# 96 token slots per expert and pass, and an expert block's four turns set singly between products of its second down item

## What is computed

```python
def swiglu(h, w_gate_up, w_down):
    g, u = jnp.split(h @ w_gate_up, 2, axis=-1)
    return (jax.nn.silu(g) * u) @ w_down

def moe_ffn(h, router, w_gate_up, w_down):
    t = h.reshape(B * S, D)                          # 256 x 1024
    logits = (t @ router).astype(jnp.float32)        # 8 experts
    top_v, top_i = lax.top_k(logits, TOP_K)          # 2 of 8 per token
    gates = jax.nn.softmax(top_v, axis=-1)
    combine = jnp.sum(jax.nn.one_hot(top_i, N_EXPERTS) * gates[..., None], axis=1)
    for e in range(N_EXPERTS):
        out = out + combine[:, e:e + 1] * swiglu(t, w_gate_up[e], w_down[e])
```

## Time and profile before

| | |
|---|---|
| median of three runs | 1441.33 us |
| span of the profiled execution | 1439.5 us |
| TensorE matmul busy | 1433.5 us (100% of the span) |
| VectorE busy | 1140.8 us (79%) |
| ScalarE busy | 964.0 us (67%) |
| GpSimd busy | 97.2 us (7%) |
| read from HBM | 434.88 MB |

### The profile page before, as it was taken

The page is one execution under the profiler, slowest core; times in us unless marked ns, Lnnn a source line. Parts: engine busy times, 40 slices in busy tenths (PEclk is TensorE's granted clock), DMA queues, the critical chain, the costliest instruction groups (busy, mean ns, idle before and its releaser), DMA issues.

```text
span 1439.5 us, 19842 instructions
## 1 busy us (share of the span) xinstructions
PE 1433.5 (100%) x6854; PEld 1205.2 (84%) x6854; DVE 1140.8 (79%) x898; ACT 964.0 (67%) x839; POOL 97.2 (7%) x146
## 2 busy tenths in 40 slices
PE   9999999999999999999999999999999999999999
PEld 9998888888998888888888888888888888888887
DVE  6486654554676698989888888998898898888897
ACT  7465444444684577777777777777777777777775
POOL 3010000000031120000000000000000000000000
PEclk9999999999999999999999999999999999999999
DMA  9454655554345599999999999999999999999995
GB/s 334 142 176 146 220 189 180 199 177 154 106 176 171 202 378 391 375 373 396 383 362 393 392 360 388 395 368 374 394 379 367 393 392 353 396 389 371 380 393 201
DMA packets 212590, 442.92 MB, mean 308 GB/s; under 512 B 16372, under 2 KB 56760, under 8 KB 212544
## 3 DMA queue, kind: packets, MB, share of 16 engines
q1 hardware_dynamic: 208640, 430.18, 81.9%
q0 software_dynamic: 3888, 12.13, 2.8%
q10 hardware_dynamic: 16, 0.00, 0.0%
HBM read 434.88 MB, written 7.37 MB: 307 GB/s over the span
## 4 chain that ended last, share of the span: by engine, by line
PE 99%; DVE 1%; ACT 0%; issue 0%; POOL 0%; DVEq 0%; ACTq 0%; POOLq 0%
PE PS L1716 21%; PE PS L1717 21%; PE PS L1720 21%; PE PS L1421 5%; PE PS L1420 5%; PE PS L1419 5%; PE PS L1150 4%; PE PS L1206 2%; PE PS L1198 2%; PE PS L1200 2%; PE PS L1257 1%; PE PS L1263 1%; PE PS L1260 1%; PE PS L1180 1%; PE PS L1705 1%; PE PS L1708 1%
## 5 line engine op out<-in xcount | busy, mean ns | idle before, releaser
L1862 DVE TENSOR_TENSOR wlo<-ring,whi 128x2048 fp32r<-128x2048 f32 x334 | 764.1, 2292 | 96.5 <-ACT whi L785 94.4
L785 ACT ACTIVATE whi<-ring 128x2048 fp32r<-128x2048 f32 x334 | 640.5, 1919 | 186.5 <-PE PS L1720 176.4
L1716 PE MATMUL PS<-whi,xhi 128*128 128x512 f32 x864 | 340.9, 395 | 0.0
L1717 PE MATMUL PS<-whi,xlo 128*128 128x512 f32 x864 | 336.6, 390 | 0.0
L1720 PE MATMUL PS<-wlo,xhi 128*128 128x512 f32 x864 | 231.0, 389 | 0.0
L1720 PEld LDWEIGHTS PS<-wlo,xhi 128*128 128x128 f32 x864 | 162.1, 188 | 33.9 <-DVE wlo L1862 0.2
L1717 PEld LDWEIGHTS PS<-whi,xlo 128*128 128x128 f32 x864 | 162.4, 188 | 32.3
L1716 PEld LDWEIGHTS PS<-whi,xhi 128*128 128x128 f32 x864 | 162.3, 188 | 32.4
L1716 PE MATMUL PS<-whi,hhi 128*128 128x512 f32 x440 | 172.0, 391 | 0.0
L1717 PE MATMUL PS<-whi,hlo 128*128 128x512 f32 x440 | 171.3, 389 | 0.0
L1829 DVE TENSOR_TENSOR wlo<-ring,whi 128x2048 fp32r<-128x2048 f32 x42 | 96.2, 2292 | 59.0 <-ACT whi L754 59.0
(11 more groups left out here) (380 smaller groups left out, 1584.8 us busy)
## 6 DMA issues: line engine op xcount, KB each, us to landing
ring<-in_moe_w_gate_up SPq DMA_DIRECT2D x448, 512.0 KB, 6.7
ring<-in_moe_w_down SPq DMA_DIRECT2D x224, 512.0 KB, 5.7
ring<-in_dense_w_gate_up SPq DMA_DIRECT2D x56, 512.0 KB, 4.5
ring<-in_dense_w_down SPq DMA_DIRECT2D x28, 512.0 KB, 3.9
ring<-in_a_w_in SPq DMA_DIRECT2D x12, 768.0 KB, 6.2
ring<-in_mem_w_kv SPq DMA_DIRECT2D x4, 1024.0 KB, 5.5
ring<-in_a_w_out SPq DMA_DIRECT2D x4, 1024.0 KB, 5.2
ring<-in_b_w_out SPq DMA_DIRECT2D x4, 1024.0 KB, 4.8
```

The source lines that it names most:

```text
L785: nc.scalar.activation(whi[:, j, :], ring[:, h * SLOT:(h + 1) * SLOT], ACT.Copy).then_inc(S("highs"), 1)
L1716: mm(out_, lhsT=xh, rhs=whi[:, j, c0:c0 + HD], start=begin, stop=False)
L1717: mm(out_, lhsT=xl, rhs=whi[:, j, c0:c0 + HD], start=False, stop=False)
L1862: v.tensor_tensor(wlo[:, j, :], ring[:, h * SLOT:(h + 1) * SLOT], whi[:, j, :].bitcast(F32), ALU.subtract).then_inc(S("lows"), 1)
```

## The change

`CAP` becomes 96, so `PASSES` becomes 3. A few small tiles whose width was `CAP` but that are also used otherwise (`Sx`, `iota`, `first_slot`) keep a width of 128, and the placing of the results (`gates`) handles a third pass with two more small VectorE operations. An expert block's four turns no longer stand behind item 5 but inside it: behind the first matmul of each of the item's four pairs one chunk is turned. The item's first matmul waits for `h_ready` too.

```diff
-CAP = 128
+CAP = 96
...
+            def turn_chunk(c):
+
+                return tr(PS[:, 3, c * CAP:(c + 1) * CAP], hnE[:, c * P:(c + 1) * P])
+
+            def expert_cut(i, b, q, j, parts, turn=None):
...
                 pe.wait_ge(S("highs"), upto(i, PERE, ECUT + m + 1))
-                for out_, xh, xl, c0, begin, end in parts:
+                if turn is not None:
+                    pe.wait_ge(S("h_ready"), turn)
+                for c, (out_, xh, xl, c0, begin, end) in enumerate(parts):
                     mm(out_, lhsT=xh, rhs=whi[:, j, c0:c0 + HD], start=begin, stop=False)
+                    if turn is not None:
+                        turned = turn_chunk(c)
+                        if c == 3:
+                            turned.then_inc(S("h_turned"), 1)
                     mm(out_, lhsT=xl, rhs=whi[:, j, c0:c0 + HD], start=False, stop=False)
...
-                        if last and b == NBE - 1:
-                            expert_down(i, b, b - 1, between=lambda: turn_expert(i * NBE + (NB + NBE)))
-                            continue
-                        expert_down(i, b, b - 1)
+                        expert_down(i, b, b - 1, i * NBE + (NB + b + 1))
                     elif not first:
                         pe.wait_ge(S("h_low"), i * NBE + NB)
-                        expert_down(i, 0, NBE - 1)
-                    if b > 0 or not first:
-                        turn_expert(i * NBE + (NB + b + 1))
+                        expert_down(i, 0, NBE - 1, i * NBE + (NB + 1))
...
+                for q in range(2, PASSES):
+                    then(v.tensor_scalar(place_at[:, 1], place_at[:, 0], float(q * CAP), float((NE - 1) * CAP), ALU.is_ge, ALU.mult))
+                    then(v.tensor_tensor(place_at[:, 2], place_at[:, 2], place_at[:, 1], ALU.add))
```

More of the change, by code:

```diff
@@ L288, in build @@
         o = 2 * NT * FB
-        Sx = carve(o, NT, CAP); o += NT * CAP
+        Sx = carve(o, NT, P); o += NT * P
         tok_f = carve(o, NT); o += NT
@@ L293, in build @@
         NC = PASSES * NE
-        iota = carve(o, CAP); o += CAP
-        iotai = arena[:, o:o + CAP].bitcast(I32); o += CAP
+        iota = carve(o, P); o += P
+        iotai = arena[:, o:o + P].bitcast(I32); o += P
         m8 = carve(o, NT, 8); o += NT * 8
@@ L301, in build @@
         picked = carve(o, NT + 1, NE); o += (NT + 1) * NE
-        first_slot = carve(o, CAP); o += CAP
+        first_slot = carve(o, P); o += P
         key = carve(o, NT); o += NT
@@ L651, in _ @@
             pool.wait_ge(S("att_out"), 1)
-            pool.iota(iotai, pattern=[[1, CAP]], base=0, channel_multiplier=0).then_inc(S("iota"), 1)
+            pool.iota(iotai, pattern=[[1, P]], base=0, channel_multiplier=0).then_inc(S("iota"), 1)
             pool.wait_ge(S("iota"), 1)
@@ L660, in _ @@
             pool.memset(blank[:, :, 0], 0.0).then_inc(S("iota"), 1)
-            pool.tensor_copy(blank[:, :, 1], iota[0:NC + 1]).then_inc(S("iota"), 1)
-            pool.tensor_scalar(blank[:, :, 2], iota[0:NC + 1], float(SEQ), None, ALU.add).then_inc(S("iota"), 1)
+            pool.tensor_copy(blank[:, :, 1], iota[0:NC + 1, 0:CAP]).then_inc(S("iota"), 1)
+            pool.tensor_scalar(blank[:, :, 2], iota[0:NC + 1, 0:CAP], float(SEQ), None, ALU.add).then_inc(S("iota"), 1)
             pool.wait_ge(S("iota"), 8)
@@ L1682, in gather @@
                         last = mm(PS[:, 6 + k // 4, (k % 4) * CAP:(k % 4 + 1) * CAP], lhsT=xn[:, t, k * P:(k + 1) * P],
-                                  rhs=Sx[:, t, :], start=(t == 0), stop=(t == NT - 1))
+                                  rhs=Sx[:, t, 0:CAP], start=(t == 0), stop=(t == NT - 1))
                     if k == KH - 1:
@@ L1693, in _ @@
             more = pe.value_load(cnt_i[0:1, 0:1], min_val=0, max_val=PASSES - 1)
-            def expert_cut(i, b, q, j, parts):
+            def turn_chunk(c):
+                return tr(PS[:, 3, c * CAP:(c + 1) * CAP], hnE[:, c * P:(c + 1) * P])
+            def expert_cut(i, b, q, j, parts, turn=None):
                 m = expert_item(i, b, q)
@@ L1731, in expert_gate_up, with expert_down @@
                          q == 3 and kk == 1) for kk in range(2) for g in range(2)])
-            def expert_down(i, b, f, between=None):
+            def expert_down(i, b, f, turn):
                 for q in (4, 5):
-                    if q == 5 and between:
-                        between()
                     _, _, j = expert_slot(i, b, q)
@@ L1740, in expert_down @@
                         (PS[0:CAP, 4 + hh, :], hhiE[:, 2 * (q - 4) + kk, :], hloE[:, 2 * (q - 4) + kk, :], kk * D + hh * HD,
-                         f == 0 and q == 4 and kk == 0, f == NBE - 1 and q == 5 and kk == 1) for kk in range(2) for hh in range(2)])
+                         f == 0 and q == 4 and kk == 0, f == NBE - 1 and q == 5 and kk == 1) for kk in range(2) for hh in range(2)],
+                        turn=turn if q == 5 else None)
             def turn_expert(n):
@@ L1746, in turn_expert @@
                 for c in range(4):
-                    last = tr(PS[:, 3, c * CAP:(c + 1) * CAP], hnE[:, c * P:(c + 1) * P])
+                    last = turn_chunk(c)
                 last.then_inc(S("h_turned"), 1)
@@ L1907, in next_dispatch @@
                     for t in range(NT):
-                        part = v.tensor_scalar(Sx[:, t], iota, put_at[:, t:t + 1], None, ALU.is_equal)
+                        part = v.tensor_scalar(Sx[0:CAP, t], iota[0:CAP], put_at[:, t:t + 1], None, ALU.is_equal)
                     part.then_inc(S("dispatch"), 1)
@@ L2411, in _ @@
             for t in range(NT):
-                last = v.tensor_scalar(Sx[:, t], first_slot, key[:, t:t + 1], None, ALU.is_equal)
+                last = v.tensor_scalar(Sx[:, t, 0:CAP], first_slot[:, 0:CAP], key[:, t:t + 1], None, ALU.is_equal)
             last.then_inc(S("dispatch"), 1)
```

## The result

The changed kernel takes 1450.09 us (median of 4 runs, 1449.62 to 1450.6) against 1441.18 us before (median of 4, 1440.73 to 1442.09): a ratio of 1.0062 with a 95% interval of 1.0049 to 1.0074. It is 8.9 us slower, where 4.3 us less were forecast. The profiled executions stand 8.6 us apart, 1448.1 against 1439.5 us.

The account below looks back on a forecast made before the run. TensorE was taken to bound the kernel. The terms -4.8 - 0.1 - 1.5 + 0.95 + 1.15 gave -4.3 us, a span of 1435.2 and a median of 1437.0 us, range 1433.0 to 1442.8.

Parts of the forecast that it names:

- What bounds the kernel: Expert stage: TensorE sets the time, its matmuls covering all 892.00 us of the window at in effect full clock.
- 96 slots in the products: Some 4000 expert products: spacing stays 0.2267 us with 96 stationary columns, cost zero; bounds no loss, gain 0.013 us each.
- rival of faster products: All products: fewer stationary columns save 0.0033 us on each of 4000, -13 us, giving 1424 us; chance 0.08.
- Lone turns: 54 groups of four turns set singly between products: 0.094 us a turn, 0.38 against 0.47 a group, -4.8 us.
- The eight turns: Eight turns of gathered rows, seven times: each 0.027 us shorter with 96 columns, -1.5 us.
- The wait in expert 0, block 1: Item 5's first product there must wait for `hnE`, as VectorE is still catching up: +0.95 us.
- The end: Last block and final down items: later turns delay the split, copy and last subtraction, so TensorE waits: +1.15 us.
- The steady blocks: Item 5 in the loop's blocks: the earlier wait for `h_ready` is met 0.16 us early, cost zero.
- The gather: Gather at the routing: its moving side shrinks by a quarter but loads run without a pause; zero, bound -1.3 us.

Follow-up runs that it names:

- the probe: Kernel before the change with extra matmuls behind its last one; its time means nothing; a lone 96-column turn cost 120 ns before 128-wide products, 86 before 96-wide ones.
- wide, grouped kernel: Changed kernel (96 slots) with turns back in a group behind item 5 and every product reading a 128-column stationary tile: 1436.61 us, ratio to before 0.9963.

## Why the prediction was wrong

The forecast was 1437.0 us in a range of 1433.0 to 1442.8; 1450.09 lies above it. Point by point:

- **What bounds the kernel: right.** TensorE fills the stage at full clock before and after.
- **96 slots in the products: wrong, and this is the step that failed.** The text took "the spacing as unchanged: zero for some 4000 products" and as bounds "no loss, and as gain" up to 0.013 us each. Measured: +0.0033 us each, +13.4 us. The argument was that the load had 0.04 us to spare, so a shorter load could give nothing. It does not follow that it could cost nothing: no row showed a product with fewer stationary columns, so nothing excluded a loss, and the bounds should have reached to that side as well. The rival of faster products named the place and had the sign the wrong way. Its mirror image, 1437 + 13 = 1450 us, is what was measured; that the sizes agree so well is luck, for the rival's 0.0033 came from a quarter of the excess over 512 columns, and the measured price follows no such rule.
- **Lone turns: right in mechanism and nearly in size.** Forecast 0.094 us a turn and -0.09 a block. Measured 0.08 from the turn to the next product and 0.086 in all in the probe, and 0.11 less a block, -5.9 us over 54 blocks. The load did shrink with its columns (162 ns at 96), as taken from the earlier trace rows. What the text credited to setting the turns singly came wholly from the 96 slots: grouped, the turns cost the same.
- **The eight turns: right.** -1.5 us forecast; block 6 of an expert stood 0.91 us above the others and now 0.66, 7 x 0.25 = -1.8 us.
- **The wait in expert 0, block 1: right place, +0.95 forecast, 0.7 measured. The end: +1.15 forecast, 1.0 measured.** The steady blocks never waited for `h_ready`, as said: at 563.59 item 5's load starts 0.28 us after `hnE` is done.
- **The gather: missed.** Taken as zero or a gain; in the two profiles the stretch around it came out about 1.2 us longer, with the half clock. That the change causes this is not shown, only that runs with 96 slots had the long stretch more often.

Sum against the two profiles: 13.4 - 5.9 - 0.1 - 1.8 + 0.7 + 1.0 + 1.2 = +8.5, measured +8.6 us. Without the first and the last term it is -6.1 us (forecast -4.3). The wide, grouped kernel has neither wait, so it should show -7.8; it shows -5.1, of which 2 us are the price of the wide tile beside the turns and the rest is of the size of the clock's effect.

## What to carry to other kernels

In a stream of loads and products, a load that is hidden is not one that may be changed at no cost: where no row shows the new pair of stationary and moving widths, leave room on both sides, for 3 ns on each of 4000 products outweighed all that the change was made of. Keep the pair that the stream runs best with (128 by 512 here) by padding the stationary tile, and take the narrowness only where it is the moving side, as in the turns. And when a wait is moved ahead of a run of work, look at the first and the last blocks of the pipeline: the steady ones had 0.16 us to spare in the old trace and 0.28 in the new, the other two places lost 1.7 us.

## What the runs showed of the hardware

- For fp32r products with 512 moving columns, 128 stationary columns were the fastest of nine widths: 226.7 ns against 228.8 to 233.5. With 448 the best were 104 and 112 (200.0 against 202.7), with 256 it was 80 (113.3 against 119.7). The recorded load got about 0.83 ns shorter with each column taken away. The cause of the uneven pattern stays open.
- A turn alone between two products cost 119 to 120 ns before a 128-column load, whether it moved 128 or 96 columns, and 86 ns when it moved 96 columns before a 96-column load.
- One program had a mean clock of 1.000, 0.998 or 0.996 in different executions, and at the lower two took 2 to 3 us longer of 1440. Profiles with these means had none, 6.8 and 10.2 us of half clock, at the same place of the program.
